# Mixture-of-experts stage: the two least loaded experts share one slot, 64 tokens each, side by side in the array's columns

## What is computed

```python
logits = xt @ w_router + b_router            # 1024 tokens, 32 experts
top_val, top_idx = lax.top_k(logits, 4)      # 4 experts for each token: 4096 pairs
gates = jax.nn.softmax(top_val, axis=-1)
# for each expert e, on the tokens that chose it:
hb = xb @ w1[e] + b1[e]                      # 1024 -> 2048
x_glu = jnp.minimum(hb[:, :1024], 7.0)
x_lin = jnp.clip(hb[:, 1024:], -7.0, 7.0)
act = x_glu * jax.nn.sigmoid(1.702 * x_glu) * (x_lin + 1.0)
out = act @ w2[e] + b2[e]                    # 1024 -> 1024
# y[token] += gate * out[token]
```

## Time and profile before

| | |
|---|---|
| median of 3 runs | 2594.08 us (2588.51 to 2594.45) |
| the profiled execution: time | 2597.89 us |
| the profiled execution: span of its core | 2596.1 us |
| TensorE busy in the span | 2418.1 us, 93% |
| phase F on TensorE, first to last matmul | 883.4 to about 2551.4 us |
| mean granted TensorE clock over the span | 0.968 |

### The profile page before, as it was taken

One profiled execution on the slowest core, in us unless ns is written; L12 is line 12 of the kernel. 1 busy time (PEld: TensorE's weight loads), 2 busy tenths in 40 slices (PEclk: granted clock), 3 DMA queues, 4 the chain that ended last, 5 costly groups with the idle time before them and its releaser, 6 DMA issues. The chain is left out here.

```text
span 2596.1 us, 29106 instructions
## 1 busy us (share of the span) xinstructions
PE 2418.1 (93%) x11256; PEld 1585.8 (61%) x11257; DVE 632.6 (24%) x1536; ACT 365.9 (14%) x825; POOL 431.4 (17%) x998
## 2 busy tenths in 40 slices
PE   7899988989896699999999999999999999999993
PEld 3445556434443485968769678587686686684441
DVE  2031165222435521212122122121121221211111
ACT  3001054011311001010110101100101111101111
POOL 3806882020010101010000100000001001000002
PEclk9999988999997899999999999999999999999996
DMA  8604111610005558586787887878878888989854
GB/s 196 162 0 65 44 16 53 163 60 0 1 1 209 196 180 243 202 265 215 270 273 249 265 272 264 268 258 273 278 256 281 287 284 281 299 282 314 283 173 146
DMA packets 373344, 508.03 MB, mean 196 GB/s; under 512 B 49032, under 2 KB 234632, under 8 KB 373205
## 3 DMA queue, kind: packets, MB, share of 16 engines
q1 hardware_dynamic: 360872, 469.43, 55.0%
q0 software_dynamic: 11008, 35.89, 6.2%
q10 hardware_dynamic: 1324, 0.83, 0.1%
HBM read 469.39 MB, written 38.77 MB: 196 GB/s over the span
## 5 line engine op out<-in xcount | busy, mean ns | idle before, releaser
L2069 PE MATMUL ps<-xT,we 128*128 128x160 f32 (+9 forms) x3584 | 516.7, 307 | 1.4 <-ACT xT L2316 1.4
L2069 PEld LDWEIGHTS ps<-xT,we 128*128 128x128 f32 x3584 | 508.5, 190 | 15.1 <-issue 8.0
L2011 PE MATMUL ps<-we,xT 128*128 128x512 f32 x1152 | 506.8, 594 | 0.0
L2011 PEld LDWEIGHTS ps<-we,xT 128*128 128x128 f32 x1152 | 213.8, 190 | 258.5 <-issue 258.5
L2083 PE MATMUL ps<-actT,we 128*128 128x160 f32 (+9 forms) x1792 | 261.1, 307 | 0.0
L2083 PEld LDWEIGHTS ps<-actT,we 128*128 128x128 f32 x1792 | 253.4, 190 | 5.6 <-DVE outT L2230 2.1
L2035 PE MATMUL ps<-we,actT 128*128 128x512 f32 x576 | 255.1, 596 | 0.7 <-ACT actT L2347 0.7
L1906 POOL DMA_INDIRECT acc_dram<-orow,sx x46 | 70.9, 1542 | 779.0 <-ACT orow L2327 487.2
L2339 ACT ACTIVATE sg<-glu 128x512 f32<-128x512 f32 (+9 forms) x92 | 49.8, 541 | 1040.7 <-DVE glu L2185 549.6
L2035 PEld LDWEIGHTS ps<-we,actT 128*128 128x128 f32 x576 | 106.6, 190 | 135.1 <-issue 134.2
L795 PE MATMUL ps<-xnT,wa 128*128 128x512 f32 x384 | 168.9, 601 | 7.6 <-DMA wa<-in_w_in 7.6
(11 more groups left out here) (333 smaller groups left out, 2143.8 us busy)
## 6 DMA issues: line engine op xcount, KB each, us to landing
we<-in_w SPq DMA_DIRECT2D x384, 1024.0 KB, 5.9
wa<-in_w_in SPq DMA_DIRECT2D x4, 2048.0 KB, 12.9
xrow<-in_x SPq DMA_DIRECT2D x32, 128.0 KB, 7.4
wa<-in_w_xkv SPq DMA_DIRECT2D x2, 2048.0 KB, 10.2
h<-in_x SPq DMA_DIRECT2D x4, 1024.0 KB
acc_dram<-h SPq DMA_DIRECT2D x1, 4096.0 KB
fin<-acc_dram SPq DMA_DIRECT2D x8, 512.0 KB, 8.9
out<-fout SPq DMA_DIRECT2D x32, 128.0 KB, 2.4
```

The lines of the kernel that those rows point to most:

```text
L2011: last = nc.tensor.matmul(m.ps[:, 2 * part + c, :], m.xT[:, 4 * half + k, 0:P], view[:, k, :], start=False, stop=(half == 1 and k == 3), s ...
L2069: last = nc.tensor.matmul(bank[:, part * WIN:part * WIN + W], view[:, k, (j % 2) * P:(j % 2 + 1) * P], m.xT[:, k, 0:W], start=(k == 0), st ...
```

## The change

Ranks 30 and 31 go into one slot, slot 1, which is now a third kind: *paired*. There are 31 slots. The paired slot gathers 64 rows of each expert into one tile of 128 partitions, and each layer runs two matmuls where a narrow slot runs one: tokens 0 to 63 (64 stationary columns) against the first expert's weights into PSUM partitions 0 to 63, and tokens 64 to 127 against the second expert's into partitions 64 to 127. Its 24 weight pieces come in turn from both experts. The bias matmuls take three rows, through a selector `sel`, since each half has a bias row of its own. Its result goes out in two scatters of 64 rows, the second after the first has landed. The gates of the second half are fetched through `high`, a copy of `gate_l` moved up by 64 partitions; SyncE issues that copy and ten small ones for `sel` at the start of phase F, and VectorE has three more steps there. The other 30 slots keep their experts' widths and form. The core of the diff (counters that run over `NS` instead of `E` are left out):

```diff
-RANK_WIDTH = (256, 224, 200, 168, 164, 164, 160, 160, 160, 156, 144, 136, 136, 132) + (P,) * 18
-RANK = tuple(r for i in range(14) for r in (i, 31 - i)) + (17, 16, 15, 14)
+RANK_WIDTH = (256, 224, 200, 168, 164, 164, 160, 160, 160, 156, 144, 136, 136, 132) + (P,) * 16 + (64, 64)
+SLOTS = ((0,), (30, 31)) + tuple((r,) for i in range(1, 14) for r in (i, 30 - i)) + ((16,), (15,), (14,))
+NS = len(SLOTS)
+PIECE0 = tuple(PIECES * sum(len(r) for r in SLOTS[:s]) for s in range(NS + 1))
...
@@ sync
+        sp.wait_ge(init_f, 8)
...
+                for i, e in enumerate(experts):
+                    load_rows(sp, m, a, s, e, row_in[s % 2], 2 * i)
+            if s == 0:
+                sp.dma_start(m.high[ST:P], m.gate_l[0:ST]).then_inc(high_in, 16)
+                for r in range(4):
+                    sp.dma_start(m.sel[32 * r:32 * r + 1, 0:ST], m.ones[0:1, 0:ST]).then_inc(high_in, 16)
+                    sp.dma_start(m.sel[32 * r + 2:32 * r + 3, ST:P], m.ones[0:1, ST:P]).then_inc(high_in, 16)
+                for r in (2, 3):
+                    sp.dma_start(m.sel[32 * r + 1:32 * r + 2, :], m.ones[0:1, :]).then_inc(high_in, 16)
+            for i in range(PIECES * len(experts)):
+                n = PIECE0[s] + i
...
+                load_piece(sp, m, a, s, i, experts[i % len(experts)])
@@ gpsimd, columns, gather and scatter
+            if paired[s]:
+                pool.wait_ge(high_in, 16 * 11)
+                for i, x in enumerate(experts):
+                    g.tensor_copy(m.gx[:, c, i:i + 1], m.idx_g[:, bass.ds(x * NB, 1)]).then_inc(idx_ok if i else low_ok, 1)
+                    g.tensor_copy(m.sx[:, c, i:i + 1], m.idx_s[:, bass.ds(x * NB, 1)]).then_inc(idx_ok if i else low_ok, 1)
+                g.tensor_tensor(m.low[:, 1:2], m.gate_l[:, bass.ds(e * NB, 1)], m.low[:, 0:1], ALU.mult).then_inc(low_ok, 1)
...
+                    for i in range(2):
+                        pool.indirect_dma_start(xg[q % 2][ST * i:ST * i + ST, :], None, a.xn_dram, ...)
...
+                    pool.indirect_dma_start(a.acc_dram, ..., orow[q % 2][0:ST, :], ...).then_inc(pair_out, 16)
+                    pool.wait_ge(pair_out, 16 * paired[:s + 1].count(True))
+                    pool.indirect_dma_start(a.acc_dram, ..., orow[q % 2][ST:P, :], ...).then_inc(scattered[q % 2], 16)
@@ tensor
+        def rows_by_weights(s, i, bank, moved, half):
+            shared = len(SLOTS[s])
+            views = []
+            for x in range(shared):
+                piece_ready(s, shared * i + x)
+                views.append(piece_view(m, s, shared * i + x))
+            for k in range(4):
+                for x, view in enumerate(views):
+                    cols = slice(ST * x, ST * x + ST) if shared == 2 else slice(0, P)
+                    last = nc.tensor.matmul(m.ps[cols, bank, :], moved[:, 4 * half + k, cols], view[:, k, :], start=False,
+                                            stop=(half == 1 and k == 3), skip_group_check=True)
...
+                k = 3 if paired[s] else 2 if r >= 2 else 1
+                last = nc.tensor.matmul(m.ps[:, r, :], (m.sel if paired[s] else m.ones)[32 * r:32 * r + k, :], m.brow[32 * r:32 * r + k, s % 2, :],
@@ vector
         v.memset(m.outT[:], 0.0).then_inc(init_f, 1)
+        v.memset(m.sel[:], 0.0).then_inc(init_f, 1)
+        v.memset(m.high[:], 0.0).then_inc(init_f, 1)
+        v.tensor_scalar(m.low[:, 0:1], m.at_row[:, 0:1], float(ST), None, ALU.is_lt).then_inc(init_f, 1)
```

More of the change, by code:

```diff
@@ L1763, in phase_f @@
     plan_x(0)
-    for s in range(E):
+    for s in range(NS):
         if s and wide[s - 1]:
@@ L1804, in out_tile @@
         return tile0[s] + half
+    rows_in = [6 * sum(len(SLOTS[t]) for t in range(s + 1) if not wide[t] and t % 2 == s % 2) for s in range(NS)]
     def piece_used(eng, n):
-        s, i = divmod(n, PIECES)
+        s = max(t for t in range(NS) if PIECE0[t] <= n)
+        i = (n - PIECE0[s]) // len(SLOTS[s])
         if i < 8:
@@ L1996, in narrow @@
                 pe.wait_ge(l1_free, free_before[s])
-            loads = sum(1 for t in range(s) if not wide[t] and t % 2 == s % 2)
-            pe.wait_ge(row_in[s % 2], 16 * 6 * (loads + 1))
+            pe.wait_ge(row_in[s % 2], 16 * rows_in[s])
+            if paired[s]:
+                pe.wait_ge(high_in, 16 * 11)
             for r in range(4):
-                k = 2 if r >= 2 else 1
-                last = nc.tensor.matmul(m.ps[:, r, :], m.ones[32 * r:32 * r + k, :], m.brow[32 * r:32 * r + k, s % 2, :],
+                k = 3 if paired[s] else 2 if r >= 2 else 1
+                last = nc.tensor.matmul(m.ps[:, r, :], (m.sel if paired[s] else m.ones)[32 * r:32 * r + k, :], m.brow[32 * r:32 * r + k, s % 2, :],
                                         start=True, stop=False, skip_group_check=True)
@@ L2007, in narrow @@
                         i = 4 * c + 2 * part + half
[L2008 to L2012, removed]
+                        last = rows_by_weights(s, i, 2 * part + c, m.xT, half)
                         last.then_inc(l1_full, 1)
@@ L2020, in narrow @@
             for n in range(2):
-                last = nc.tensor.matmul(m.ps[:, 4 + n, :], m.ones[32 * n:32 * n + 1, :], m.crow[32 * n:32 * n + 1, s % 2, :],
+                k = 3 if paired[s] else 1
+                last = nc.tensor.matmul(m.ps[:, 4 + n, :], (m.sel if paired[s] else m.ones)[32 * n:32 * n + k, :], m.crow[32 * n:32 * n + k, s % 2, :],
                                         start=True, stop=False, skip_group_check=True)
@@ L2031, in narrow @@
                     i = 8 + 2 * half + n
[L2032 to L2037, removed]
+                    rows_by_weights(s, i, 4 + n, m.actT, half).then_inc(l2_full, 1)
         def second_free(s):
@@ L2341, in _ @@
         glu_of = [JF if x else 2 for x in wide]
-        glu_before = [sum(glu_of[:s]) for s in range(E + 1)]
+        glu_before = [sum(glu_of[:s]) for s in range(NS + 1)]
         def act_out(s, c):
```

125 lines of the change are left out of this document (73 added, 52 removed).

## The result

| | before | after |
|---|---|---|
| median | 2594.06 us (2588.51 to 2594.45, 4 runs) | 2546.68 us (2542.97 to 2552.4, 4 runs) |
| the profiled execution: time | 2597.89 us | 2542.97 us |
| its span | 2596.1 us | 2541.3 us |
| phase F, from the first clearing step to the start of the last matmul | 1680.7 us | 1632.5 us |
| slot 1 on TensorE | 49.5 us (narrow) | 50.7 us (paired) |

The ratio is 0.9824, with a 95% interval of 0.9801 to 0.9847: 47 us, 1.8% less. The forecast was 2550 us, range 2544 to 2562. The changed kernel was timed once more beside the kernel before, with a ratio of 0.9815 (0.9786 to 0.9844).

The account below looks back on a forecast made before the run. TensorE's instruction stream was taken to bound phase F. The terms -45.9 + 1.4 + 0 + 0.3 = -44.2 us took the profiled 2597.9 to 2553.7, a median of 2550 us, range 2544 to 2562.

Parts of the forecast that it names:

- The narrow slot: Phase F: if the paired slot costs TensorE what a narrow one does, one whole narrow slot goes, -45.9 us.
- The halves side by side: Paired slot: two 64-column matmuls run at the same time, so its weight matmuls cost a narrow slot's 41.4 us.
- Changes of form: Paired slot: TensorE enters the halved array form six times, at 0.24 us each, +1.4 us.
- Weights: Paired slot: the ring hides the doubled weight demand at 327 GB/s, cost 0, upper bound +10 us.
- Start of phase F: Before the first gather: VectorE's three new steps +0.9, less an earlier second gather; +0.3 us taken.
- the right collision: Start of phase F: two weight pieces share DMA with the gathers; delayed 6 us, the second gather may come 1.49 earlier.
- The median: Whole run: the profiled execution before is 3.8 us above the median, so 2553.7 becomes a median of 2549.9.
- Weights late: Rival, paired slot: a hidden weight transfer shows, 2 to 10 us, 2552 to 2560; chance 0.08.
- loads in the open: Rival, paired slot: one or two stationary loads exposed per pair of records, +13 or +26 us, 2563 to 2576; chance 0.03.
- halves in turn: Rival, paired slot: halves run one after the other at 512 columns, 41.4 us come back, 2591; chance 0.04.
- The slower one: Rival, ranks 30 and 31: an expert of 65 tokens runs the overflow loop, about +95 us, 2645; chance 0.02.

Follow-up runs that it names:

- the run with halves: The kernel before, with each weight matmul of all 18 narrow slots split into two of 64 columns against the same weights: 2619.13 us.
- the run with 8 buffers: The changed kernel with a ring of 8 weight buffers instead of 14, 8 pieces ahead of phase F instead of 12: 2557.13 us.

## Why the prediction was right, point by point

The forecast of 2550 us was 3.3 us from the median, and the mechanism was the one named.

- **The narrow slot, -45.9.** Right. From the start of slot 2 on, phase F is 45.8 us shorter, with the 0.1 us by which slot 2 grew.
- **The halves side by side, at 0.43 us a pair of records.** Right, and rightly read from L952: a form that the kernel used elsewhere for 64 and 128 columns had the same rate at 512. What I had not asked is how far apart the two may stand in the program.
- **Changes of form, +1.4.** 1.2, and 1.2 again in the slots behind wide ones of the run with halves. The even price of 0.24 us a round is not right in its parts: rounds between narrow slots cost 0.13 us in the mean, so those about the transposes of result rows cost more.
- **Weights, 0, hidden by the ring.** Right. The reckoning by the piece gave the run with 8 buffers +8 to +12, and its slots 1 and 2 grew by 9.0 together; but only 6.8 of that are waits, the share in slot 2 (3 us) didn't come, and the first wait came at 21 us rather than 27. So that agreement is in part luck. The DMA engines moved 357 GB/s with a backlog, not the 327 that I took; that was the cautious side.
- **Start of phase F, +0.3, between -0.6 and +0.9.** Wrong: -1.6, and another -1.9 behind it. The step that failed is the sum of VectorE's steps and the gather. I had the three new steps at 0.9 us; they cost 0.4 (the step after the first one starts 2.36 us behind it instead of 1.93, and the last of them is as much later). I had the right collision, but charged it only to the second gather; it also held up the first. The pieces went out 10.8 us later than before, not 6: the eleven copies took 0.6 us each to issue, where I had 0.4, and by then both gathers had landed. So TensorE's transposes begin 12.6 us into the phase instead of 13.2, in spite of VectorE's steps, and the second batch follows the first without a wait for its gather. And I left out that less idle time at 1.2 GHz may move the rise of the clock. With the terms as measured, -45.9 + 1.2 - 1.6 - 1.9 + 0.1 is -48.1 us, phase F's own difference. The forecast for it was -44.2; with the clock rising late it would have been -45.4. That 2550 lies 3.3 us from the median is the sum of these misses, and the range of 2544 to 2562 held it.
- **The median.** I set the sum against the profiled execution of before and took its 3.8 us of distance from the median as they were. The scatter lies in phases A to E, as the further traces show, and it was right to carry the difference over unchanged.
- **The rivals.** Weights late, loads in the open and halves in turn did not come about. The slower one had the right point (the token beyond the room) and a wrong price: 393 us, not 95. I priced its work and not its search; a loop of 256 windows was there to be read in the code.

## What to carry to other kernels

When two stationary operands of at most 64 columns meet streams of 512, put their outputs in the two halves of the PSUM partitions and let them alternate, or go in runs of at most two matmuls; here both streams then cost one, since the data for two arrived. Whether they arrive is a sum over the buffers in stock and the rate with a backlog, not a comparison of rates: here 610 GB/s were wanted in the halved stretches, 357 delivered, and nothing was late with 14 buffers, while the slot was 9 us longer with 8. And look at what is issued just ahead of a phase's first gather: transfers that nobody waits for cost 2 us there.

## What the runs showed of the hardware that I had not expected

- TensorE started a matmul of the idle column half while up to three earlier records of the busy half were queued (the reading that fits all four orders): 51.0 us with runs of two matmuls, 62.0 with four, 71.5 with eight, 50.7 in turn.
- Two matmuls of 64 columns over all 128 rows didn't slow each other at 512 streamed columns: 7.02 us for 32 records, against 6.9 to 7.0 for 16 alone.
- A loop turn with one register load and one branch took 1.3 us on TensorE and at most 1.2 on VectorE, so a rare case found behind 240 others cost 315 us before TensorE did anything for it.
- The clock's rise at the start of a phase came 16.9 or 23.6 to 23.9 us in, with the same transposes ahead of it, and the difference was worth 1.5 to 2.8 us of slot 0 (83.9 us against 85.4 to 86.7).
